# A decoder layer in float32 on one core: the running maximum's rows, moved from the end of the second attention block to the end of the third

## The reference

```
h = RMSNorm(x); z = h @ W_in
A: sliding-window attention (window 128), 8 heads, sinks, relative bias
B: mLSTM, 4 heads, exact per token, with a running maximum as stabiliser:
   b = cumsum(log_forget);  m_t = max(b + m, max over s <= t of (b_t - b_s + ig_s))
   D = exp(b_t - b_s + ig_s - m_t);  inter = exp(b + m - m_t)
   w = exp(b_last - b + ig - m_new); h = (inter q C + (q k * D) v) / max(|den|, exp(-m_t))
x = x + W_out [RMSNorm(A) || RMSNorm_per_head(sigmoid(o) * h)]
x = x + W_down relu(RMSNorm(x) W_up)^2;  y = RMSNorm(x)
```

## Time and profile before

| what | us |
|---|---|
| median of 3 runs | 2432.26 (2429.77 to 2432.62) |
| the profiled execution, its own time | 2429.19 |
| its span | 2427.4 |
| TensorE busy | 2378.6 (98%) |
| VectorE busy | 1359.0 (56%) |
| ScalarE busy | 961.3 (40%) |
| mean granted TensorE clock | 0.997 of full |

### The profile page before, as it was taken

The page is one execution under the profiler, slowest core; times in us unless marked ns, Lnnn a source line. Parts: engine busy times, 40 slices in busy tenths (PEclk is TensorE's granted clock), DMA queues, the critical chain, the costliest instruction groups (busy, mean ns, idle before and its releaser), DMA issues.

```text
span 2427.4 us, 33523 instructions
## 1 busy us (share of the span) xinstructions
PE 2378.6 (98%) x13125; PEld 2017.0 (83%) x13125; DVE 1359.0 (56%) x3109; ACT 961.3 (40%) x2049; POOL 75.9 (3%) x131
## 2 busy tenths in 40 slices
PE   7999999999999999999999999999999999999998
PEld 6988788888897888888998888888889879888886
DVE  4478544546368654446356854444656765444444
ACT  4345433334345533334334543333433544233331
POOL 1000000000000000000000400000010000000000
PEclk9999999999999999999999999999999999999999
DMA  6312323233411232334421233323343112222221
GB/s 182 86 45 85 97 96 96 96 113 120 145 54 53 87 98 93 97 95 131 147 67 36 71 102 96 96 95 113 118 130 110 47 49 93 79 79 79 81 85 57
DMA packets 178266, 224.35 MB, mean 92 GB/s; under 512 B 18123, under 2 KB 129044, under 8 KB 178092
## 3 DMA queue, kind: packets, MB, share of 16 engines
q1 hardware_dynamic: 165596, 189.82, 25.5%
q10 hardware_dynamic: 6560, 22.55, 2.6%
q0 software_dynamic: 5952, 9.83, 1.5%
HBM read 210.78 MB, written 12.60 MB: 92 GB/s over the span
## 4 chain that ended last, share of the span: by engine, by line
PE 93%; DVE 4%; issue 1%; ACT 1%; DMA 0%; ACTq 0%; DVEq 0%
PE ps L1881 28%; PE ps L1883 28%; PE ps L1882 28%; PE ps L1960 2%; PE ps L1940 1%; PE ps L1949 1%; DVE w_lo L1095 1%; PE ps L2006 1%; DVE w_lo L1099 1%; PE ps L2009 1%; PE ps L1921 1%; PE ps L1909 0%; PE ps L1985 0%; DVE wide L1479 0%; PE ps L2016 0%
## 5 line engine op out<-in xcount | busy, mean ns | idle before, releaser
L1881 PE MATMUL ps<-a_hi,w_hi 128*128 128x512 f32 (+2 forms) x1704 | 592.2, 348 | 11.6 <-DVE w_lo L1095 5.9
L1883 PE MATMUL ps<-a_hi,w_lo 128*128 128x512 f32 (+2 forms) x1704 | 593.6, 348 | 0.0
L1882 PE MATMUL ps<-a_lo,w_hi 128*128 128x512 f32 (+2 forms) x1704 | 591.7, 347 | 0.0
L1883 PE MATMUL ps<-w_hi,u_lo 128*128 128x512 f32 (+1 forms) x1088 | 429.0, 394 | 0.0
L1881 PE MATMUL ps<-w_hi,u_hi 128*128 128x512 f32 (+1 forms) x1088 | 428.9, 394 | 0.0
L1882 PE MATMUL ps<-w_lo,u_hi 128*128 128x512 f32 (+1 forms) x1088 | 426.2, 392 | 0.0
L665 ACT ACTIVATE w_hi<-w_raw,gains 128x256 fp32r<-128x256 f32 (+1 forms) x576 | 252.9, 521 | 418.5 <-PE ps L1883 418.5
L1881 PEld LDWEIGHTS ps<-a_hi,w_hi 128*128 128x128 f32 x1704 | 322.5, 189 | 55.0 <-DVE w_lo L1099 5.3
L1882 PEld LDWEIGHTS ps<-a_lo,w_hi 128*128 128x128 f32 x1704 | 320.8, 188 | 41.0
L1883 PEld LDWEIGHTS ps<-a_hi,w_lo 128*128 128x128 f32 x1704 | 321.1, 188 | 39.4
L1103 DVE TENSOR_TENSOR x<-x,ps 128x512 f32<-128x512 f32 x272 | 185.4, 685 | 278.1 <-PE ps L1883 278.0
(11 more groups left out here) (323 smaller groups left out, 2159.7 us busy)
## 6 DMA issues: line engine op xcount, KB each, us to landing
w_raw<-in_w_up_dram SPq DMA_DIRECT2D x128, 512.0 KB, 3.7
w_raw<-in_w_down_dram SPq DMA_DIRECT2D x128, 512.0 KB, 3.5
w_raw<-in_w_out_dram SPq DMA_DIRECT2D x32, 512.0 KB, 3.5
w_raw<-in_w_in_dram SPq DMA_DIRECT2D x24, 580.0 KB, 5.0
w_raw<-in_w_in_dram SPq DMA_DIRECT2D x24, 512.0 KB, 3.8
w_raw<-in_w_in_dram SPq DMA_DIRECT2D x32, 256.0 KB, 3.1
x<-in_x_prompt_dram ACTq DMA_DIRECT2D x12, 512.0 KB, 6.7
wide<-in_x_prompt_dram ACTq DMA_DIRECT2D x12, 512.0 KB, 4.6
```

What stands on the lines that cost most here:

```text
L1881: eng.matmul(out, lh, rh, start=(k == ks[0]), stop=False)
L1882: eng.matmul(out, lh, rl, start=False, stop=False)
L1883: ins = eng.matmul(out, ll, rh, start=False, stop=(k == last))
```

## The change

`running_max` is cut in two. Its first part (the copy and the four steps of `mp`) stays at the end of the second block. Its second part, now `row_lines`, is called at the end of the third block. No instruction is added or removed.

```diff
                 for j in range(BLK):
                     eng.scalar_tensor_tensor(mp[:, j + 1:j + 2], Mrow[:, j, P - 1:P], mp[:, j:j + 1], brow[:, j, P - 1:P], ALU.max, ALU.add).then_inc(vec.sem, 1)
                     eng.wait_ge(vec.sem, vec.next(q))
+
+            def row_lines(q):
+
+                buffers = (Mrow, grow, brow, None)
                 stabilise(q, BLK, P, mp[:, 0:BLK].unsqueeze(2).broadcast_to([HM, BLK, P]), buffers, Mrel, lambda r: rows[r:r + HM, :, :], r_rows, vec)
...
                     tm_split(o - 3, 3)
                     if j == 1:
                         running_max(q)
+                    if j == 2:
+                        row_lines(q)
```

## The result

| kernel | median of the runs, us | runs |
|---|---|---|
| before | 2431.41 (2429.2 to 2433.2) | 7 |
| changed | 2438.30 (2437.5 to 2440.87) | 7 |

The ratio is 1.003, with a 95% interval of 1.0019 to 1.0042: slower by some 7 us. The profiled execution of the changed kernel took 2437.5 us, against 2429.19 before; each is the fastest of its set, so these two differ by 8.3 us where the medians differ by 6.9.

The account below looks back on a forecast made before the run. TensorE's queue of matmuls bounds the kernel, so VectorE order matters only through TensorE's waits. Loss 8.8 + 0.4, less gain 4.5, is 4.7; plus 3.0 for the clock, 7.7 us: 2440.0 us against 2432.26, range 2435.5 to 2443.0.

Parts of the forecast that it names:

- What the change moves and what stays: End of second block: five small instructions on `mp` stay; seven others, 4.63 us in a row, move.
- The gain, 4.5 us: Third block of each quarter: VectorE free earlier, TensorE's wait of about 1.13 us goes, four times.
- The loss, 8.8 + 0.4 = 9.2: Fourth blocks: copy and L1966 late, 2.94 us in quarters 1, 2 and 4 (8.8), 0.4 in the third.
- The transfers at nothing: GpSimd's line transfers start later, but their reader L1981 leaves more than 7 us of cover: no cost.
- The clock, 3.0 us: Behind new 2.9 us waits TensorE's clock falls to 1.2 GHz for 3.4 us, 1.5 us lost each; two falls counted.
- the bounds: Clock cost behind the three long waits: from nothing to 4.5 us, or twice that if a fall lasts double.
- Two of three: Clock falls taken behind two of the three new 2.9 us waits, held likely, not certain, behind each: 3.0 us.
- the forecast's own range: Whole kernel with two or three falls (+7.7 to +9.2 us): 2438.5 to 2442.5 us, chance 0.60.
- the rival with one fall or none: Clock behind the new waits holds or falls once: +4.7 to +6.2 us, 2437.0 to 2438.5; chance 0.22.
- That transposes ahead of a wait make every long wait fall: Transposes not counting as busy, all three waits pay: +9.2, up to +13.7 us; chance 0.07 beyond three simple falls.
- That falls are already paid before at the 1.2 us waits: Old third-block waits usually bring falls that now go, returning 1.5 to 3 us: +4.7 or less; chance 0.07.
- The free place: VectorE's idling before the fourth block's copy covers the move, leaving only the gain: -4.5 us, 2427.8; chance 0.04.

Follow-up runs that it names:

- three at the end: Kernel before with the last three of the seven instructions moved to the end of the third block: 2426.78 us, ratio 0.9987 to before.
- three in the gap: Kernel before with the last three of the seven instructions moved behind the third block's zT copy: 2427.51 us, ratio 0.9988 to before.
- the five moved: Kernel before with five of the seven instructions moved to the end of the third block, two staying: 2431.91 us, ratio 1.0003 to before.
- the double delay: Changed kernel plus 15 useless VectorE instructions behind its seven at the end of the third block: 2463.90 us, ratio 1.0135 to before.
- two sets of the changed kernel: Changed kernel run again unaltered, besides its first set: second set 2439.38 us, ratio 1.004 to before.
- the delay alone: Kernel before plus 15 useless VectorE instructions at the end of the third block, running maximum left in place: 2445.26 us, ratio 1.006 to before.
- the third quarter only: Kernel before with the change made in the third quarter alone, other quarters in the old order: 2429.10 us, ratio 0.9994 to before.

## Why the prediction was right

*What the change moves and what stays.* Seven instructions, 4.63 us: the same to the hundredth at the new place.

*The gain, 4.5 us.* Third blocks have no wait any more; three at the end and three in the gap show this gain by itself, -4.1 and -3.3 us, both with intervals below 1.000.

*The loss, 8.8 + 0.4 = 9.2.* Expected 2.94, 2.94, 0.4 and 2.94; measured 2.89, 2.89, 0.39 and 2.89, 9.1 in all. That VectorE has no slack there but its 1.60 us of idling is shown by the five moved (3.2 us moved, 1.46 late), the three moved (1.8 us, about 0.16 late) and the double delay (9.3 us, 7.6 late): each is late by its length less some 1.7.

*The transfers at nothing.* GpSimd's first line transfer now starts at 152.54 and the last of eight at 156.16; their reader starts at 165.89, and still waits for `cols`. GpSimd's timeline:

```profile
152.54 0.54 POOL L551 DMA_DIRECT2D Mline<-DT  x1 [86.65 <-DVE ST L1103]
...
156.16 0.52 POOL L551 DMA_DIRECT2D Mline<-ST  x1
```

and TensorE's timeline:

```profile
165.89 0.47 PE L1987 MATMUL ps<-Mline,ones_row 2*128 2x512 f32 x1 [0.61 <-ACT cols L671]
```

*The clock, 3.0 us.* The price of a fall of 3.4 us was sized rightly (1.5, measured 1.54). That a fall can last longer stood only in the bounds; that one can come without a wait was in neither. Two of three was a guess between bounds, and that the sum came so close with it is in part luck: of the 3 us that the first profile lost to falls which the trace before hasn't, half fell in the sample's work and not behind a wait. The profiled executions show one and two behind the long waits. The medians lie 2.4 and 4.0 us above the waits, one and a half to two and a half falls, though some of this may be falls elsewhere, which I can't count in runs without a trace. The total of 7.7 us came out as 6.9 and 8.5. The absolute time, 2440.0, was reckoned from a median of 2432.26 in three runs; the median of seven is 2431.41, half of the 1.7 us by which it was off. The 2438.30 measured lies, narrowly, below the forecast's own range (from 2438.5) and in that of the rival with one fall or none; the time lost, 6.9 us, lies above that rival's 6.2. So the time does not choose between them. The traces do, and they show both: one fall behind the three waits in the first, two in the second.

*The rivals.* That the clock holds is out, as a rule for all executions; one fall only is within what was seen. That transposes ahead of a wait make every long wait fall is out: 1.91 us of them stood ahead of each of the waits of 2.9 to 3.2 us, and behind four of nine (two sets of the changed kernel and the delay alone) the clock held. Whether they add anything to a wait stays open, since no run has such a wait without them. That falls are already paid before at the 1.2 us waits is not borne out: none of eleven such waits in three traces has one, and the two kernels without these waits spread over 3.9 and 6.3 us all the same. The free place was not open for 4.63 us; for work under about 1.7 us it would have been.

My argument leaned on a wait of 2.4 us (L1909) "without" a fall. That was chance. The same wait has a fall behind it in the traces of the three in the gap and of the third quarter only, and the one of 2.15 has none in those.

## What to carry to other kernels

Work that nobody needs soon still delays what is queued behind it on its engine. Before moving it, subtract from its length the idling of that engine just ahead of the next instruction that another engine waits for: here 1.60 us, so 4.63 us cost 2.9 us, and 1.8 us cost 0.16. Where the work is a chain of separate instructions, cut it to the gaps: all seven together made TensorE wait 1.2 us at the end of the second block and 2.9 at the end of the third; in two groups, four at the end of the second block and three in a gap of the third, they made it wait for nothing.

## What the runs showed of the hardware

The granted clock after a wait of TensorE is not settled by the wait's length alone. Waits of 1.2 to 1.5 us: no fall behind any. Of 2.9 to 3.2: five of nine. Of 4.0: three of three, one of double length. Of 5.1: the one there was on `both`. Of 7.6: three of three, 10.2 us each. The wait ahead of the first product, 4.3 to 5.3 us, had a fall at it in all ten traces, of 3.4 us in five and of 6.8 us in five. I had expected one length of stretch and one price. The Trainium skill (TensorE: Matmul & The Clock Gate, section "Why this matters for your kernels") asks to avoid longer idle gaps between bursts of matmuls. These counts agree with it. My prediction had read it as a rule for any gap, by which all three waits would pay; the page speaks of gaps above a length, which my prediction left out. Here a short wait may pay too: behind the one of 2.15 us (L1638 of the last quarter) the clock fell in seven of ten traces, behind the one of 2.4 us in two.

The clock also fell with no wait at all. At 1794.4 in the changed kernel it stood at 0.50 for 3.4 us, right behind 6 us of the sample's small matmuls (64 rows or 32 columns), in which TensorE counts as busy throughout. The trace of before has the same work and no fall. Six of the ten traces have a fall there, one of them of double length. What decides it, no run shows. Runs of one kernel part by such falls: with three at the end, the four runs with a mean clock of 0.997 took 2425.98 to 2426.18 us, the three with 0.995 took 2428.33 to 2429.87.
